# Two blocks on one core: the small matrix inverse of the gated delta rule is reordered between five engines

## The reference, cut to what matters

```
qkv = silu(causal_conv4(hn @ w_in[:, :3072]))       # q, k, v: 8 heads of 128
g   = -exp(a_log) * softplus(a + dt_bias);  beta = sigmoid(b)
A   = strict_lower((k*beta) @ k.T * decay)          # per head and chunk
u,w = solve(I + A, [v*beta, k*beta*exp(g)])         # triangular, unit diagonal
v'  = u - w @ S;  o = (q*exp(g)) @ S + tril(q @ k.T * decay) @ v'
S   = S*exp(g_last) + (k*exp(g_last - g)).T @ v'
x   = x + (rms(o) * silu(z)) @ w_out
```

## Time and profile before

| what | value |
|---|---|
| median of three executions | 845.68 us |
| the profiled execution's own time | 847.66 us |
| its span | 845.9 us |
| TensorE busy | 819.2 us (97%) |
| VectorE busy | 597.5 us (71%) |
| ScalarE busy | 488.8 us (58%) |
| GpSimd busy | 41.1 us (5%) |
| DMA | 153.83 MB, mean 182 GB/s |

### The profile page before, as it was taken

The page is one execution under the profiler, slowest core; times in us unless marked ns, Lnnn a source line. Parts: engine busy times, 40 slices in busy tenths (PEclk is TensorE's granted clock), DMA queues, the critical chain, the costliest instruction groups (busy, mean ns, idle before and its releaser), DMA issues.

```text
span 845.9 us, 18071 instructions
## 1 busy us (share of the span) xinstructions
PE 819.2 (97%) x7670; PEld 797.0 (94%) x7670; DVE 597.5 (71%) x1045; ACT 488.8 (58%) x762; POOL 41.1 (5%) x63
## 2 busy tenths in 40 slices
PE   7999989699999999999999999999999999999998
PEld 7899979589999999999999999999999999999998
DVE  4786865477898787696889885555777877575662
ACT  5756547355665665564444454346777767777731
POOL 0500000006300000000000000200000000000000
PEclk9999989799999999999999999999999999999999
DMA  7362226642876654457566673893466444444450
GB/s 284 123 234 100 106 100 136 141 150 93 246 271 230 237 213 169 150 203 285 210 225 240 233 247 128 215 286 122 153 229 217 157 169 174 150 145 156 148 177 26
DMA packets 26496, 153.83 MB, mean 182 GB/s; under 512 B 2848, under 2 KB 3376, under 8 KB 12080
## 3 DMA queue, kind: packets, MB, share of 16 engines
q1 hardware_dynamic: 24432, 146.37, 48.9%
q0 software_dynamic: 1984, 6.31, 4.2%
HBM read 150.04 MB, written 2.62 MB: 180 GB/s over the span
## 4 chain that ended last, share of the span: by engine, by line
PE 84%; DVE 7%; ACT 3%; issue 3%; DMA 2%; SPq 0%; DVEq 0%; ACTq 0%
PE ps L481 83%; DMA raw<-weights 2%; DVE wlo L1406 1%; ACT whi L989 1%; PE ps L847 1%; DVE early L1473 1%; DVE early L1565 1%; DVE ada_ring L1487 1%; PE ps L700 0%; ACT L978 0%; DVE hlo L1434 0%; DVE arena L1438 0%; DVE arena L1473 0%; DVE olo L1451 0%; ACT hhi L1019 0%
## 5 line engine op out<-in xcount | busy, mean ns | idle before, releaser
L1406 DVE TENSOR_TENSOR wlo<-raw,whi 128x1024 fp32r<-128x1024 f32 x224 | 267.0, 1229 | 130.1 <-ACT whi L989 130.0
L481 PE MATMUL ps<-hhi,whi 128*128 128x256 f32 x1024 | 295.2, 288 | 7.1 <-DVE hlo L1432 2.9
L481 PE MATMUL ps<-hlo,whi 128*128 128x256 f32 x1024 | 290.4, 284 | 0.9 <-issue 0.9
L481 PE MATMUL ps<-hhi,wlo 128*128 128x256 f32 x1024 | 290.1, 283 | 0.0
L989 ACT ACTIVATE whi<-raw 128x1024 fp32r<-128x1024 f32 x224 | 227.4, 1055 | 89.2 <-PE ps L481 61.5
L481 PEld LDWEIGHTS ps<-hhi,whi 128*128 128x128 f32 x1024 | 196.6, 192 | 10.3 <-issue 7.8
L481 PEld LDWEIGHTS ps<-hlo,whi 128*128 128x128 f32 x1024 | 196.7, 192 | 1.5 <-issue 1.1
L481 PEld LDWEIGHTS ps<-hhi,wlo 128*128 128x128 f32 x1024 | 196.6, 192 | 0.0
L481 PE MATMUL ps<-ohi,whi 128*128 128x256 f32 x448 | 129.0, 288 | 1.5 <-DVE olo L1451 1.2
L481 PE MATMUL ps<-ohi,wlo 128*128 128x256 f32 x448 | 126.7, 283 | 0.0
L481 PE MATMUL ps<-olo,whi 128*128 128x256 f32 x448 | 126.7, 283 | 0.0
(11 more groups left out here) (222 smaller groups left out, 962.8 us busy)
## 6 DMA issues: line engine op xcount, KB each, us to landing
raw<-weights SPq DMA_DIRECT2D x112, 1024.0 KB, 4.9
ada_ring<-ada SPq DMA_DIRECT2D x24, 1024.0 KB, 5.0
arena<-bias_rows_d POOLq DMA_DIRECT2D x4, 512.0 KB, 14.1
x<-x_t SPq DMA_DIRECT2D x2, 512.0 KB, 4.6
bias_rows_d<-early POOLq DMA_DIRECT2D x1, 1024.0 KB, 12.1
arena<-bias_rows_b POOLq DMA_DIRECT2D x4, 256.0 KB, 7.7
arena<-bias_rows_d POOLq DMA_DIRECT2D x4, 256.0 KB, 16.9
out_t<-x SPq DMA_DIRECT2D x4, 256.0 KB, 2.5
```

Of the source, the lines that this page charges most:

```text
L481: return pe.matmul(o, l, r, start=start, stop=stop, skip_group_check=skip)
L1406: dve.tensor_tensor(wlo[:, unit % UNITS, :, :], raw[:, c % RAW, 4 * half:4 * half + 4, :], whi[:, unit % UNITS, :, :].bitcast(F32), ALU.su ...
```

## The change

It makes five edits. (1) The tiles of jobs 8 and 9 are grouped differently between the matrix steps, masks 2 and 3 are put together, and two more tiles of job 9 stand ahead of `first_products(0)`. (2) In the levels ScalarE splits the whole next chunk at the start of a level, VectorE does its `low` first, and `take_values` moves from ScalarE to VectorE. The splits and the convolution of job 8 come earlier on both engines. (3) Three modulation sums instead of two stand in the levels: sum 0 at level 4, sum 1 at level 5 behind `take_halves`, sum 2 ahead of the copies at L1604; the one at chunk 23 goes, and counters move by one. (4) GpSimd's first wait for `conv_ok_sem` goes (the one at L419 stays). (5) The write of the bias rows waits for `nt_ok_sem` 4 instead of `t_ok_sem` 5.

```diff
-ADA_AT = [14, 15, 23, 25, 27, 29, 31, 33, 35, 42, ...
-ADA_EARLY = 2
+ADA_AT = [13, 14, 15, 25, 27, 29, 31, 33, 35, 42, ...
+ADA_EARLY = 3
...
-            if lv == 6:
-                turn_order.append("mod0")
+            if lv >= 5:
+                turn_order.append(f"mod{lv - 5}")
...
-            pool.wait_ge(conv_ok_sem, 1)
             pool.wait_ge(lmask_in_sem, 16)
...
-            pool.wait_ge(t_ok_sem, 5)
+            pool.wait_ge(nt_ok_sem, 4)
             pool.dma_start(scr_d[0:32].rearrange("p h t -> h p t"), ...
...
             products(1, 0)
-            parts(8, 0, 2)
+            parts(8, 0, 4)
+            products(1, 1)
             masked(0)
-            parts(8, 2, 3)
             masked(1)
-            products(1, 1)
-            parts(8, 3, 5)
-            decay_rows(2)
-            products(2, 0)
+            parts(8, 4, 8)
+            for p in (2, 3):
+                decay_rows(p)
+                products(p, 0)
+                products(p, 1)
+            parts(9, 0, 2)
             masked(2)
-            products(2, 1)
-            parts(8, 5, 6)
-            decay_rows(3)
-            products(3, 0)
             masked(3)
-            products(3, 1)
-            parts(8, 6, 8)
-            parts(9, 0, 1)
+            parts(9, 2, 4)
...
             first_products(0, 256).then_inc(tp_ok_sem, 1)
-            parts(9, 1, 8)
+            parts(9, 4, 8)
...
-                if last:
-                    ada(0, taken(slot_of_mod(0)))
+                if lv >= 5:
+                    ada(lv - 5, taken(slot_of_mod(lv - 5)))
                 parts(J, 0, 4)
...
             state_decay(1)
+            high(9)
             decay(0)
             decay(1)
-            high(9)
+            first_tap(8)
             state_decay(2)
+            state_decay(3)
             decay(2)
-            state_decay(3)
             decay(3)
-            first_tap(8)
             high(10)
+            silu(8)
...
-                high(J + 1, range(1))
+                high(J + 1)
...
-                high(J + 1, range(1, 2))
-                if 2 <= lv <= 5:
-                    take_values(lv - 2)
-                if lv == 1:
-                    silu(8)
...
+            low(9)
             pair_matrices(0)
             pair_matrices(1)
-            low(9)
+            conv(8)
             pair_matrices(2)
...
             take_rows(0)
-            conv(8)
             low(10)
             for lv in range(1, LEVELS - 1):
+                low(10 + lv)
                 if lv == 1:
...
-                low(10 + lv)
+                    dve.wait_ge(ce_sem, 2)
+                else:
+                    take_values(lv - 2)
                 if lv < 5:
                     take_rows(lv)
                 else:
-                    dve.wait_ge(sil_ok_sem, 1)
-                    pair_sums(0)
                     take_halves()
                 if lv <= 3:
                     conv(8 + lv)
-            pair_sums(1)
-            mod_of_slot(0)
+                if lv == 4:
+                    dve.wait_ge(sil_ok_sem, 1)
+                    pair_sums(0)
+                if lv == 5:
+                    mod_of_slot(0)
+                    pair_sums(1)
+            mod_of_slot(1)
+            pair_sums(2)
```

More of the change, by code:

```diff
@@ L60, in chunks_of @@
     return [JOB_OUT_D + 4 + 2 * (job - JOB_OUT_D) + h for h in range(2)]
-ADA_AT = [14, 15, 23, 25, 27, 29, 31, 33, 35, 42, 44, 46, 48, 50, 52, 54, 56, 58, 60, 62, 78, 82, 86, 90]
-ADA_EARLY = 2
+ADA_AT = [13, 14, 15, 25, 27, 29, 31, 33, 35, 42, 44, 46, 48, 50, 52, 54, 56, 58, 60, 62, 78, 82, 86, 90]
+ADA_EARLY = 3
 def laid_at(c):
@@ L541, in ada_after @@
                             pe.wait_ge(pT_v_sem, 2 * (4 + (J - JOB_D) // 4))
-                        pe.wait_ge(mod_ok_sem, n - 1)
+                        pe.wait_ge(mod_ok_sem, n - 2)
                         ada(n)
@@ L842, in turn @@
                         if soft0 == 4 and hh and 1 <= i < 5:
-                            pe.wait_ge(mod_ok_sem, 19 + i)
+                            pe.wait_ge(mod_ok_sem, 18 + i)
                         if soft0 + i:
@@ L1502, in mod_of_slot, with take_values @@
                 take_mod(n, b, free)
+            def take_values(i):
+                b, free, n = slot(slot_of_values(i))
+                dve.wait_ge(vT_ok_sem, i + 1)
+                for c in range(2):
+                    for hh in range(2):
+                        k = 8 * c + 2 * i + hh
+                        m = dve.tensor_scalar(vr[:, 4 * i + 2 * c + hh, :], b[:, (2 * c + hh) * P:(2 * c + hh) * P + P], hc[:, 4, k:k + 1], None, ALU.mult)
+                m.then_inc(free, 1)
             dve.wait_ge(ones_ok_sem, 6)
@@ L1777, in gains_of_c @@
             def gains_of_c():
-                dve.wait_ge(slot(slot_of_mod(0))[1], slot(slot_of_mod(0))[2] + 1)
-                dve.wait_ge(mod_ok_sem, 7)
+                for n in range(ADA_EARLY - 1):
+                    dve.wait_ge(slot(slot_of_mod(n))[1], slot(slot_of_mod(n))[2] + 1)
+                dve.wait_ge(mod_ok_sem, 6)
                 scaled_gain(0)
@@ L1858, in _ @@
             finish_c(3, 1)
-            dve.wait_ge(mod_ok_sem, 11)
+            dve.wait_ge(mod_ok_sem, 10)
             add_x(JOB_OUT_C, gate=16, before_last=lambda: take_mod(19))
-            dve.wait_ge(mod_ok_sem, 19)
+            dve.wait_ge(mod_ok_sem, 18)
             scaled_gain(1)
@@ L1870, in _ @@
             attend(JOB_D, 8, 4, A(bias_at, 16, 384), True)
-            dve.wait_ge(mod_ok_sem, 23)
+            dve.wait_ge(mod_ok_sem, 22)
             add_x(JOB_OUT_D, gate=40)
```

## The result

The changed kernel takes 856.57 us (median of 4, 851.89 to 865.34), the kernel before 845.89 us (4, 845.35 to 847.66) beside it: ratio 1.0125 [1.0078, 1.0172]. A second time, on another chip, it was 857.88 us (854.43 to 860.99) against 848.11, ratio 1.0109 [1.0052, 1.0167]. It is slower, by some 10 us in these two comparisons. All 23 executions on record for it have a median of 856.91 us, or 855.05 without the two longest (865.08 and 865.34), which count as slow runs; against the 848.1 to 848.7 us of the kernel before in later runs that is 6 to 9 us. The forecast was +3.8 us and 849.5 us, with 855 as the upper end: the sign was right, the size was not, and the measured time lies outside the range. The executions of the changed kernel also lie 13 us apart, those of before 2 us in that comparison and up to 9 us in later ones; the one profiled took 852.53 us, so it shows the less bad half.

The account below looks back on a forecast made before the run. TensorE, busy nearly everywhere, was taken to set the pace, with some instruction-fetch stops. Terms: -10.3 + 2.5 + 11.0 - 0.9 + 1.5 = +3.8 us, put on the 845.7 us median for 849.5 us; range 838 to 855.

Parts of the forecast that it names:

- item 2: TensorE's 4.14 us stop at 155.79 us, at the transposes, goes because the bias writes are no longer there: -4.14 us.
- items 1, 3: TensorE's wait for VectorE's copy at L1576 goes, -3.37 us; the lower clock from 152.5 us on goes, -1.6 us.
- item 5: New wait ahead of the first small products, 2.2 us, plus 0.3 at the next level: +2.5 us.
- costs nothing: Order of projections and small products before the levels, shorter Pool chain, moved waits on modulation counters: 0 us.
- items 7, 8, 9: Early bias writes hold up an instruction fetch, +11.0 us; earlier 0.87 and 2.48 us stops shrink, -0.9; lower clock after stops, +1.5.
- item 4: Small gains: GpSimd's earlier mask work ends the 0.74 us stop at 38.87, and some 0.5 us in the levels: -1.2 us.
- Item 6: One more pair sum, 3.5 us of VectorE, before the copies for TensorE's last stage: hidden by 0.8 us, taken as 0.
- rival B: Fetch held only to the first write's end, about t + 12.3; stop 4.4 us instead of 11.0; 842.9 us, chance 0.18.
- Rivals C: Two instruction requests are caught under the writes, 15.5 us instead of 11.0: 854 us, chance 0.12.
- D: The third ada load is late at the end of the levels and TensorE waits: 841.4 us, chance 0.12 with others.

Follow-up runs that it names:

- write at 62 us: Bias-row writes moved to the sixth convolution mark: 845.99 us (0.9972) on the kernel before; 847.43 us (0.9979) on the changed kernel with GpSimd's first wait put back.
- ada(0) moved: First ada product set behind its level's tiles, on the changed kernel with GpSimd's wait back, writes at 61.8 us and masks behind their products: 841.10 us, again 839.40.
- without edit 4: Changed kernel with GpSimd's first wait for the first convolution put back, bias writes still early: 853.75 us, ratio 1.0056 to the kernel before.
- edit 4 alone: Kernel before with only GpSimd's first wait for the first convolution removed: 850.39 us, ratio 1.003.
- second profile: Profile from the repeat of the unmodified changed kernel on another chip (median 857.88 us); the profiled execution took 860.99 us.

## Why the prediction missed

The step that failed is the pricing of what the change adds and takes away. The sum gave the held-up fetch its largest size as if it came in every execution (+11.6, measured 6.1), and took the late write's stop at full size too (-4.1, measured -2.1); it put the early ada product at nothing (measured +3.2), and GpSimd's freed work at a gain (-0.7, measured +2.3 alone and +4.4 here, not resolved). The differences between the experiments' medians give each term a measured value:

| term of the forecast | forecast | measured | from |
|---|---|---|---|
| write gone from its late place (item 2) | -4.1 | -2.1 | before with the write at 62 us |
| L1576, lower clock, levels (items 1, 3, half a us of 4) | -5.5 | -5.1 | the remainder |
| mask wait (item 5) | +2.5 | +3.3 | masks put behind their products |
| ada(0) ahead of its tiles ("costs nothing") | 0 | +3.2 | ada(0) moved |
| write in front of narrow blocks (items 7, 8, 9) | +11.6 | +6.1 | without edit 4, write early against at 62 us |
| GpSimd's wait gone (item 4) | -0.7 | +4.4 | edit 4 undone |
| sum | +3.8 | +9.8 | |

The sum is the changed kernel's second comparison, +9.8. The remainder is what is left of the write at 62 us on the changed kernel (+1.4 against the same on the kernel before) when the 3.3 and 3.2 are taken off, so the table closes by construction; each other row is a difference of two medians, each against the kernel before on its own chip. By the intervals on record such a row is good to 2 to 6 us, the last one least.

1. *Items 1 and 3, right.* No wait at L1576, full clock behind it. The 9.1 against 9.2 us held.
2. *Item 2, half.* The stop went. But 4.14 us is what one execution showed; in the trace of edit 4 alone, with the writes as late, it is not there. So the late place has two outcomes as well, and the 2.1 us by medians lies between none and 4.14. How often each comes no run shows, nor what the lower clock that stayed has to do with it.
3. *Item 4, the sign wrong: 3.0 us by edit 4 alone, 5.1 by the table.* The prediction looked at the one collision that goes (0.74 us at 38.87 did go) and counted "the shorter Pool chain" among the steps that cost nothing. The work that starts earlier has to run beside something. It runs beside the two-input instructions of the first layer norm, on the only path that TensorE has at that time: 2.09 us by the rows, in the first profile after and in that of edit 4 alone (21.91 and 22.05 against 19.82). And of the 0.74 us that it was to win 0.62 came back as another stop. Alone the edit costs 2.3; the 4.4 of the table is within noise of that.
4. *Item 5, right.* 2.56 us for 2.2 (its own 3.3 less 1.4 make 1.9, not 2.2), and with the lower clock behind it 3.3 by medians; in the first profile the lower clock behind it cost another 2.7.
5. *The ada product, missed: 3.2 us.* Item 6 checked the new sum against the copies at the end. It never asked where TensorE's own instruction for sum 0 stands now: at level 5 ahead of the tiles, while VectorE's sum is done 1.31 us after TensorE gets there. The 3.2 us are measured with the write at 62 us, where the lower clock followed; in both profiles of the changed kernel it didn't, and the place costs 1.7.
6. *Items 7 to 9: mechanism right, size an average over two outcomes.* Border, place and the 11 us are as forecast in two of four traces with the early writes (11.98 and 11.87); a third has 2.21 there and 9.00 at the next border, again 11 us in all. In the fourth, the first profile, rival B's packet came at 111.0 us, 12.3 us behind the last pair of matrices (98.7) as that rival said, and TensorE went on at 113.42, t + 14.7 for its t + 14.6; the stop is 2.17 and not 4.4 us because the lower clock behind the mask wait had delayed TensorE's own arrival (t + 12.5 for t + 10.1). The forecast took one row of before as the rule. The mean of its own forecast and B, 7.7 us, would have been nearer to the 6.1 and 6.4 by medians; that the two come equally often no run shows.

Misses 3 and 5 together, +8.3, less the +5.5 given too much at 7 to 9, and 3.2 more on items 2 (2.0), 1 and 3 (0.4) and 5 (0.8), make the 6.0 us between +3.8 and +9.8. The direction was right through the term that was too large, and so in part by luck.

Rivals C and D did not show: no trace has two long stops back to back of 15 us, and none a wait for the third ada load (item 6, hidden as forecast).

## What to carry to other kernels

Whoever removes a wait must say what the freed work now runs beside, above all on the path to the first operands. When a result is asked for earlier on one engine, look up where its consumer stands in the order of the other one: a wait of 1.3 us cost 1.7 to 4.6. A long stop seen in one execution may be missing in the next: before it is put into a sum, take a second profile. And long DRAM writes issued by GpSimd belong beside wide matmuls: the same two writes cost 6 us more ahead of the narrow blocks than at 62 us, where no stop of TensorE stands behind them until 96 us.

## What was not expected of the hardware

- A wait of 1.3 us on TensorE was followed by 6.8 us at granted clock 0.50 with the write at 62 us, and by clock 1.00 in both profiles of the changed kernel. There also is a stretch at the lower level with no idle time before it. The same 24 matmuls, first before (clock 1.00) and then after (0.57 from 75 to 79 us):

```profile
73.09 2.94 PE L481 MATMUL ps<-arena 128*128 128x128 f32 x24
```

```profile
75.23 4.46 PE L480 MATMUL ps<-arena 128*128 128x128 f32 x24
```

They take 4.57 us with edit 4 alone, in the order of before, and 2.94 in the changed kernel without edit 4, so TensorE's order doesn't decide it. It is a loss of 1.5 us that no term of the forecast and no row of the table holds.

- Under two GpSimd-issued writes of 1 and 0.5 MB no instruction packet moved for up to 19 us (from 101 to 120 us in the second profile). By the block borders the one that was missing had been asked for at about 105.5 us, so it waited some 14.5 us. SP's loads were held up too, but only while the first write ran: one had been issued at 107.03 us, and from 109 to 111 us just the writes' queue moved.

```profile
q0 software_dynamic: 47, 0.19, 90.3%
```

Then 144 load packets moved beside the second write, and the instruction packet still did not. Once the packet had moved, TensorE went on after 2.2 to 2.4 us each time (111.0 to 113.42, 117.2 to 119.61, 120.0 to 122.41). The Trainium skill (DMA: Bandwidth & Descriptors, "Queues, rings and completion order") has an engine take its rings in turn; for SP's loads beside the second write the trace agrees, for those under the first write and for the instruction queue it does not, by some 4 and 14.5 us.
